# The branch phase of a two-layer hybrid decoder step: the four decode steps of a round one after the other, then four half-chunks in a row

## What is computed

```python
hp = rms_norm(xp, norm_g[l])
q, k, v, ga, logf, u, vb, gb, g_a, g_b = in_proj(hp, w_in[l], ...)
attn = fox_prompt(q, k, v, logf)                       # for the samples: fox_sample, below
s_sgu = sgu_prompt(vb, w_s[l], b_s[l])
a = attn * jax.nn.silu(gate_a)
b = u * s_sgu * jax.nn.silu(gate_b)                    # u = gelu(...)
m = jax.nn.sigmoid(g_a) * (a @ w_pa) + jax.nn.sigmoid(g_b) * (b @ w_pb)
x = x + m @ w_o
```

```python
s_past = einsum('bqhd,bkhd->bhqk', q, kp) * scale + (c_new[..., :, None] - c_past[..., None, :])
s_new  = einsum('bqhd,bkhd->bhqk', q, k) * scale + (c_new[..., :, None] - c_new[..., None, :])
p = softmax(concatenate([s_past, where(causal, s_new, -inf)]))
out = einsum('bhqk,bkhd->bqhd', p[..., :P], vp) + einsum('bhqk,bkhd->bqhd', p[..., P:], v)
```

## Time and profile before

| | us |
|---|---|
| median of 3 runs | 2015.58 |
| lowest, highest | 2014.07, 2018.64 |
| the profiled execution | 2014.72 |
| its span in the profile | 2013.0 |

### The profile page before, as it was taken

How to read it: one execution, slowest core, us unless ns; L and a number is a source line. 1 busy time by engine, 2 the same in 40 slices (tenths; PEclk the granted TensorE clock), 3 DMA queues, 4 the chain that set the end, 5 groups by cost and what they waited for, 6 DMA issues and landing times.

```text
span 2013.0 us, 30982 instructions
## 1 busy us (share of the span) xinstructions
PE 1919.7 (95%) x11188; PEld 1762.0 (88%) x11188; DVE 973.0 (48%) x2298; ACT 672.8 (33%) x1487; POOL 511.7 (25%) x523
## 2 busy tenths in 40 slices
PE   5999899999898999999999999999998999999998
PEld 4999898999877889998789988999997788999986
DVE  5546556554165334545445565656532643454431
ACT  5344344444133222113224344444432332231120
POOL 3623233332021112211135242333320211131010
PEclk7999999999999999999999999999999999999999
DMA  5231313123215222524324113131321253226151
GB/s 155 65 101 48 83 50 97 49 73 87 68 38 145 75 83 81 194 82 156 104 57 120 45 46 97 42 95 48 95 69 55 52 155 94 62 74 224 49 177 52
DMA packets 217803, 178.39 MB, mean 89 GB/s; under 512 B 50260, under 2 KB 191076, under 8 KB 217652
## 3 DMA queue, kind: packets, MB, share of 16 engines
q1 hardware_dynamic: 217652, 176.41, 30.4%
HBM read 131.65 MB, written 44.71 MB: 88 GB/s over the span
## 4 chain that ended last, share of the span: by engine, by line
PE 76%; DVE 9%; issue 5%; DMA 3%; ACT 3%; SPq 1%; POOL 1%; POOLq 0%; ACTq 0%; DVEq 0%
PE bank L76 21%; PE bank L77 20%; PE bank L78 20%; PE bank L1306 2%; PE bank L1319 2%; PE bank L2071 1%; PE bank L1289 1%; PE bank L1320 1%; PE bank L1291 1%; PE bank L2094 1%; DVE at_prob L1186 1%; DVE at_ptlo L1202 1%; PE bank L1266 1%; DVE sg_sT L1534 1%; DMA me_stage<-in_w_proj_b 1%
## 5 line engine op out<-in xcount | busy, mean ns | idle before, releaser
L76 PE MATMUL bank<-keep_hhi,at_fhi 128*128 128x384 f32 (+1 forms) x768 | 260.2, 339 | 3.3 <-ACT at_th L954 3.3
L77 PE MATMUL bank<-keep_hlo,at_fhi 128*128 128x384 f32 (+1 forms) x768 | 253.5, 330 | 0.0
L78 PE MATMUL bank<-keep_hhi,at_flo 128*128 128x384 f32 (+1 forms) x768 | 253.4, 330 | 0.0
L76 PE MATMUL bank<-aw_whi,keep_hhi 128*128 128x384 f32 (+3 forms) x576 | 198.3, 344 | 1.9 <-POOL aw_wlo L252 1.2
L76 PE MATMUL bank<-keep_hhi,bw_whi 128*128 128x384 f32 (+1 forms) x576 | 196.3, 341 | 0.5 <-DVE br_th L1958 0.5
L77 PE MATMUL bank<-aw_wlo,keep_hhi 128*128 128x384 f32 (+3 forms) x576 | 195.7, 340 | 0.0
L78 PE MATMUL bank<-aw_whi,keep_hlo 128*128 128x384 f32 (+3 forms) x576 | 195.7, 340 | 0.0
L1000 ACT ACTIVATE at_prob<-at_prob,at_nmx 128x128 f32<-128x128 f32 (+7 forms) x128 | 99.5, 777 | 280.1 <-DVE at_nmx L1193 279.8
L77 PE MATMUL bank<-keep_hlo,bw_whi 128*128 128x384 f32 (+1 forms) x576 | 189.4, 329 | 0.0
L78 PE MATMUL bank<-keep_hhi,bw_wlo 128*128 128x384 f32 (+1 forms) x576 | 189.1, 328 | 0.0
L1202 DVE TENSOR_TENSOR at_ptlo<-bank,at_pthi 128x512 fp32r<-128x512 f32 x192 | 106.2, 553 | 156.7 <-ACT at_pthi L1010 156.7
(11 more groups left out here) (252 smaller groups left out, 4398.1 us busy)
## 6 DMA issues: line engine op xcount, KB each, us to landing
at_stage<-in_w_in SPq DMA_DIRECT2D x160, 128.0 KB, 2.5
mg_gate<-gates SPq DMA_DIRECT2D x32, 544.0 KB, 5.2
gates<-at_th SPq DMA_DIRECT2D x64, 192.0 KB, 2.4
br_stage<-in_w_in SPq DMA_DIRECT2D x40, 256.0 KB, 3.3
at_stage<-in_w_in SPq DMA_DIRECT2D x48, 192.0 KB, 2.6
at_decay<-ncum SPq DMA_DIRECT2D x16, 512.0 KB, 3.9
br_k<-in_cache_k SPq DMA_DIRECT2D x32, 256.0 KB, 3.1
br_v<-in_cache_v SPq DMA_DIRECT2D x32, 256.0 KB, 3.1
```

What stands on the lines that cost most here:

```text
L76: nc.tensor.matmul(out, sh, mh, start=start and i == 0, stop=False)
L77: nc.tensor.matmul(out, sh, ml, start=False, stop=False)
L78: last = nc.tensor.matmul(out, sl, mh, start=False, stop=stop and i == n - 1)
```

## The change

The four decode steps of a round stand together at its start, in the order K, Q, R, V; then come its four halves. Before, one half stood behind K, one behind Q, one behind V and one behind R. The loads LV move up with V. In the last round O comes ahead of the four halves too. No instruction is added, removed or altered.

```diff
             plan.append(("K", slot))
             if slot + NK < DB:
                 plan.append(("LK", slot + NK))
-        half()
         if 0 <= slot - 1 < DB:
             plan.append(("Q", slot - 1))
-        half()
-        if 0 <= slot - 3 < DB:
-            plan.append(("V", slot - 3))
-        half()
         if 0 <= slot - 2 < DB:
             plan.append(("R", slot - 2))
         if 0 <= slot - 3 < DB:
+            plan.append(("V", slot - 3))
             if slot - 3 + NV < DB:
                 plan.append(("LV", slot - 3 + NV))
         if slot == DB + 2:
             plan.append(("O",))
-        half()
+        for _ in range(4):
+            half()
     while halves:
         half()
```

## The result

| | before | after |
|---|---|---|
| median of 20 runs each, us | 2016.44 | 2022.37 |
| lowest to highest, us | 2012.52 to 2021.49 | 2017.42 to 2027.08 |
| profiled execution, us | 2014.72 | 2027.08 |

The ratio is 1.003, with a 95% interval of 1.0021 to 1.0039. The time lies above the range. The profiled execution of after is the slowest of its 20, 4.7 us over their median, while that of before is 1.7 us under its median.

The account below looks back on a forecast made before the run. The prediction took TensorE's busy time as the bound. Seven sets of joins at 0.23 us plus 0.09 where V meets O gave 1.7 us a layer, 3.4 in two layers: 2012.2 us from the median 2015.58, range 2008.2 to 2018.2.

Parts of the forecast that it names:

- What bounds the kernel: Whole kernel: TensorE busy for 95% of the span, with no wait in the rounds that the change could remove.
- The exponential's wait: ScalarE's exponential waiting for R: falls from 54.8 us to under 10, a gain worth 0.
- The sum of the steps: A round's K, Q, R and V with their joins: 6.73 us in place of 6.96, 0.23 us less.
- K to Q: Join from K's 128*128 to Q's 128*64 on TensorE: taken at 0.10 us, what Q pays now.
- Q to R: Join from Q's last matmuls to R on TensorE: taken at 0.05 us.
- R to V: Join from R's small matmuls to V on TensorE: taken at 0.05 us.
- the drain at a change of tiling mode: At the three joins: each would cost 0.10 us by this rule, so the change would bring 2.0 us.
- dear joins: Rival at the joins between steps: 0.20 us each, 2.4 us more in all, time 2018.0 us; chance 0.13.
- the clock among the rivals: Behind rows of small matmuls: granted clock falls to 0.50, 17.6 us lost, time 2029.8 us; chance 0.07.
- The rule on transposes: K and R: transposes don't count as a busy TensorE in the same way, which would speak for the clock's fall.
- new wait on TensorE: Rival in the rounds: TensorE waits on VectorE's stream, 1 us in half the rounds, 10 us slower; chance 0.03.
- free joins: Rival at the joins between steps: they cost nothing, 6.4 us less in all, time 2009.2 us; chance 0.25.

Follow-up runs that it names:

- V twice: Against the kernel before: V's eight 16-column matmuls done twice, V still between two halves; 2070.65 us in one execution.
- K four times: Against the kernel before: K's eight 128x128 transposes done four times, K still between two halves; 2058.38 us in one execution.
- K V Q R: Against after: the row's steps reordered to K, V, Q, R, then four halves; 2012.74 us in one execution.

## Why the prediction was wrong, point by point

**What bounds the kernel** stood: TensorE without waits in the rounds, and none came. The exponential's wait fell by more than half, not under 10 us as I had said, since it now stands for VectorE's maximum in the middle of the row; it cost nothing either way.

**The sum of the steps** stood: 6.75 us for a row against 6.73. Its joins were distributed otherwise. K to Q cost 0.11, as taken. Q to R cost nothing: Q lasts 3.56 as before, R 0.32. R to V cost 0.11 (V 1.81 in place of 1.70), since V's first load of 128 columns is no longer hidden: it starts with V's own first matmul, at 711.11. Together 0.22 for 0.20. So all of the gain is in the join of Q and R. Round 6 shows it: 14.67 us before, 14.65 with K Q and R V joined but Q and R apart, 14.45 with K Q R joined and V apart, and 14.45 in after. The rule of the Trainium skill, "TensorEngine Tiling (Array Packing)", "Key Properties", on the drain at a change of tiling mode holds at two of the three joins, with 0.11 each, and the third, 64*64 to 64*128, shows nothing. The rounds' gain, without the falls, was 1.60 us a layer, 3.2 together where the sum had 3.4. (The range's upper edge stands there as 2018.2 for dear joins, whose own time was 2018.0; the result is above both.)

**The step that failed** is the one that put the clock among the rivals at 0.07. As the prediction had it: "Against it: the clock is 1.00 over today's round, and over 372 to 376 us, where TensorE was busy for only 2.58 of 4 us". Both rows are true and neither bears on the question. In today's round V has a half on either side, and a busy share says only that an instruction is under way: the profile has TensorE busy for 6.66 of the 6.66 us of the row at 706 us, behind which the clock fell, and V twice was busy for 3.49 of 3.49 us and lowered the clock, V with 16 columns behind a load of 128x128. The change put V next to R and Q's small parts, and I weighed this by its length (6.7 us) and its busy share, not by what the array had to do in it.

The rival's own price was off in both directions: 1.1 us each in all 16 rounds, 17.6 us; it was 1.56 us each in some of them, 4 and 5 of the 16. The count: after is 5.9 us slower in the median, and 3.2 were gained, so the losses are 9.1 us, or 5.8 falls an execution. The two profiles have 4 and 5, which account for 3.1 and 4.6 of the 5.9 us, the gain taken off. The one or two falls that are missing may be the spread between executions or lie outside the rounds; this I can't show.

The rule on transposes that I cited for this rival (the Trainium skill, "TensorE: Matmul & The Clock Gate", "Part 4: PE-mode transpose") finds no support as it stands: 3.4 us of fp32 transposes and nothing else, 16 times, lowered nothing. That is a clock at 1.00 that stayed there; whether transposes alone would raise a lowered one, no run here shows. With K's transposes between R and V there was one fall in ten rounds, without them four in ten, which doesn't speak for the rule either.

The other rivals: no new wait on TensorE; no free joins; none as dear as 0.20.

## What to carry to other kernels

Work that loads full weights for few columns did no harm here in small doses between dense matmuls (1.7 us, 64 places, no fall) and did in large ones (3.5 us, 16 places, 13 falls) or in a row with other thin work (12 rounds, 4 and 5 falls): the granted clock can fall behind it, and the dense work pays, at half speed for about 3.4 us each time. So before gathering small steps to save the changes of mode between them (here 0.2 us a round, against 1.56 us a fall), look at what they do per weight load, not at TensorE's busy share, and keep the thinnest of them next to dense work. Read the granted clock by stretch behind each such place in more than one profile, since a fall comes in some rounds and not in others.

## What the runs showed of the hardware that I had not expected

- The granted clock fell to 0.50 while TensorE and its weight loading were both busy for 100% of the time: 13 stretches with V twice (3.49 us of 16-column matmuls), none with K four times (3.41 us of 128-column transposes), none with 5.29 us of Q's matmuls.
- A single fall of the clock lasts about 3.4 us here and costs 1.54 to 1.58 us, by the same rounds with and without one.
- From 64*64 weights to 64*128 there is no cost to see, from 128*128 to 128*64 and from 64*64 to 128*128 there is 0.11 us. From K to V, both 128*128 in fp32, there is none: in K V Q R, K lasts 0.87 us until V starts.
- Two executions of one kernel differ in where the clock falls: at 243 and 847 us in one profile of after, in neither place in the other.
